# Two layers of a transformer encoder on one core: the down projection of pairs 2 to 7 in blocks of seven products

## The reference, cut to what matters

```python
for l in range(DEPTH):                       # DEPTH = 2
    xp = xp + token_mix(rmsnorm(xp, norm_mix[l]), ...)
    xp = xp + swiglu(rmsnorm(xp, norm_ffn[l]), w_ff_gate[l], w_ff_up[l], w_ff_down[l])
def swiglu(h, wg, wu, wd):
    return (jax.nn.silu(h @ wg) * (h @ wu)) @ wd
```

## Time and profile before

| | |
|---|---|
| Time, median of three runs | 2314.57 us |
| Time of the profiled execution | 2312.65 us |
| Its span, first to last instruction | 2310.9 us |
| PE busy | 98% of the span |
| DVE, ACT, POOL busy | 56%, 37%, 43% |
| Feed-forward stages | about 719 to 1156 us and 1860 to 2294 us |
| Mean granted TensorE clock | 0.997 of full speed |

### The profile page before, as it was taken

How to read it: one execution, slowest core, us unless ns; L and a number is a source line. 1 busy time by engine, 2 the same in 40 slices (tenths; PEclk the granted TensorE clock), 3 DMA queues, 4 the chain that set the end, 5 groups by cost and what they waited for, 6 DMA issues and landing times.

```text
span 2310.9 us, 39749 instructions
## 1 busy us (share of the span) xinstructions
PE 2262.2 (98%) x15086; PEld 2178.7 (94%) x15086; DVE 1305.1 (56%) x2330; ACT 847.1 (37%) x1650; POOL 988.0 (43%) x992
## 2 busy tenths in 40 slices
PE   8999999999999999999999999999999999999997
PEld 7998998888999999999999999978889999999997
DVE  7998553334226935727589975433332477275374
ACT  4115233444213534525420152334442245254352
POOL 5554454222564342333465445532326643333231
PEclk9999999999999999999999999999999999999998
DMA  5351121111223222322244411211112322223121
GB/s 193 104 175 62 51 73 55 37 40 35 91 100 97 68 92 65 96 70 84 65 137 149 122 56 57 70 51 37 38 42 92 109 87 83 72 84 100 65 86 61
DMA packets 70565, 187.87 MB, mean 81 GB/s; under 512 B 19824, under 2 KB 22480, under 8 KB 69392
## 3 DMA queue, kind: packets, MB, share of 16 engines
q1 hardware_dynamic: 62608, 165.64, 22.7%
q10 hardware_dynamic: 7808, 20.16, 2.6%
HBM read 173.47 MB, written 14.14 MB: 81 GB/s over the span
## 4 chain that ended last, share of the span: by engine, by line
PE 81%; DVE 16%; issue 2%; ACT 1%; DMA 0%; SPq 0%; DVEq 0%; ACTq 0%
PE gemm L712 37%; PE gemm L1182 16%; PE gemm L1172 13%; DVE side L1959 7%; PE side L1182 3%; PE side L1172 2%; PE side L1055 2%; PE side L1035 1%; PE side L818 1%; PE side L986 1%; PE side L1042 1%; DVE prod L1868 1%; DVE h_lo L1822 1%; DVE act L2298 1%; DVE act_lo L2308 1%
## 5 line engine op out<-in xcount | busy, mean ns | idle before, releaser
L685 POOL TENSOR_TENSOR ring_lo<-w_raw,ring_hi 128x512 fp32r<-128x512 f32 x236 | 319.5, 1357 | 552.4 <-ACT ring_hi L1648 552.4
L666 POOL CAST w_hi<-w_raw 128x384 fp32r<-128x384 f32 x376 | 222.8, 593 | 711.4 <-PE gemm L712 667.3
L668 POOL TENSOR_TENSOR w_lo<-w_raw,w_hi 128x384 fp32r<-128x384 f32 x376 | 450.1, 1197 | 30.1
L712 PE MATMUL gemm<-h_hi,w_hi 128*128 128x320 f32 x1616 | 405.9, 332 | 5.0 <-DVE h_lo L1822 3.8
L712 PE MATMUL gemm<-h_hi,w_lo 128*128 128x320 f32 x1616 | 368.9, 309 | 0.0
L712 PE MATMUL gemm<-h_lo,w_hi 128*128 128x320 f32 x1616 | 368.4, 309 | 0.0
L712 PEld LDWEIGHTS gemm<-h_hi,w_hi 128*128 128x128 f32 x1616 | 274.1, 189 | 36.6 <-issue 17.2
L712 PEld LDWEIGHTS gemm<-h_hi,w_lo 128*128 128x128 f32 x1616 | 270.5, 188 | 0.0
L712 PEld LDWEIGHTS gemm<-h_lo,w_hi 128*128 128x128 f32 x1616 | 270.5, 188 | 0.0
L1182 PE MATMUL gemm<-act_hi,ring_hi 128*128 128x320 f32 x864 | 267.2, 309 | 1.1 <-DVE prod L2285 1.1
L1182 PE MATMUL gemm<-act_hi,ring_lo 128*128 128x320 f32 x864 | 267.0, 309 | 0.0
(11 more groups left out here) (330 smaller groups left out, 4387.9 us busy)
## 6 DMA issues: line engine op xcount, KB each, us to landing
w_raw<-in_ws_ff SPq DMA_DIRECT2D x120, 512.0 KB, 3.4
w_raw<-in_ws_gate SPq DMA_DIRECT2D x64, 512.0 KB, 3.4
w_raw<-in_ws_in SPq DMA_DIRECT2D x44, 512.0 KB, 3.5
w_raw<-in_ws_proj SPq DMA_DIRECT2D x64, 256.0 KB, 2.6
w_raw<-in_ws_out SPq DMA_DIRECT2D x16, 512.0 KB, 3.4
w_raw<-in_ws_fd SPq DMA_DIRECT2D x16, 384.0 KB, 3.1
x_park<-x ACTq DMA_DIRECT2D x2, 2560.0 KB, 12.4
x<-x_park ACTq DMA_DIRECT2D x4, 1280.0 KB, 5.9
```

What stands on the lines that cost most here:

```text
L666: eng.tensor_copy(w_hi[s][:, cols], w_raw[s][:, cols]).then_inc(w_high.sem, 1)
L668: eng.tensor_tensor(w_lo[s][:, cols], w_raw[s][:, cols], w_hi[s][:, cols].bitcast(F32), ALU.subtract).then_inc(w_split.sem, 1)
L685: eng.tensor_tensor(lo, src, hi.bitcast(F32), ALU.subtract).then_inc(lo_plain.sem, 1)
L712: mm = eng.matmul(dst[:, hf, 0:HALF], w, r[k][:, cols] if r in (xu_hi, xu_lo) else r[:, k, cols], start=first and k == 0 and part == 0, st ...
```

## The change

The flow of the feed-forward part becomes a table, `FF_FLOW`: the gate and up blocks of pair 2; the plain down units of tiles 0 to 3; pairs 3 and 4; four **down blocks** over pairs 2, 3, 4; pairs 5, 6, 7; four down blocks over pairs 5, 6, 7; pairs 8, 9, 10; the plain down units of tiles 16 to 21.

A down block computes two output tiles (2i and 2i+1) from three pairs, by seven products. Its inner dimension is three tiles for each half, so a product is 3 x 3 = 9 matmuls and a block 63; its operands have 384 columns, not 512. Its activation blocks are made of f: for each of pairs 2 to 7 the end of the up block now makes four sums of f (S3, S1, S2, S4, VectorE, 128x320), seven high parts (ScalarE) and seven low parts (three on GpSimd: A11, A22, A12; four on VectorE), in place of two high and two low parts of 128x640. Which engine makes the low part of a weight operand is also a table, `POOL_OPS`: in gate and up blocks GpSimd keeps operands 0 and 3, and operand 6 goes to VectorE; in down blocks GpSimd has 0, 3, 4 and 6.

```diff
-FF_CHUNKS = (8, 8, 6)
+FF_FLOW = (("pair", 2), ("units", 0, 4), ("pair", 3), ("pair", 4), ("downs", (2, 3, 4)),
+           ("pair", 5), ("pair", 6), ("pair", 7), ("downs", (5, 6, 7)),
+           ("pair", 8), ("pair", 9), ("pair", 10), ("units", 16, 6))
+POOL_OPS = {"gate": (0, 3), "up": (0, 3), "down": (0, 3, 4, 6)}
...
 # TensorE
+    def block_product(v, i, dst, name, fresh):
+        tiles, wh, wl = weights(v.n + i)
+        for k in range(tiles):
+            if v.kind == "down":
+                hi, lo = f_hi[v.pairs[k], name][:, :], f_lo[v.pairs[k], name][:, :]
+                if v.out == 0 and name in POOL_LOWS:
+                    eng.wait_ge(block_pool.sem, ...)
+                elif v.out == 0:
+                    eng.wait_ge(block_dve.sem, ...)
...
 # ScalarE, quad(v): follows = the block before is an up block of pairs 2 to 7, split = this one is
     copied(QX, QY)
     cast(n + 5)
+    if follows:
+        block_high_made(b.pair, A12)
...
     copied(QW, QZ)
     cast(n + 6)
+    if follows:
+        block_high_made(b.pair, S1)
+        block_high_made(b.pair, S4)
...
     cast(n + 9)
+    if split:
+        block_high_made(v.pair, A11)
     done(5)
     cast(n + 10)
+    if split:
+        block_high_made(v.pair, A22)
+        block_high_made(v.pair, S3)
     done(6)
     cast(n + 11)
+    if split:
+        block_high_made(v.pair, S2)
...
 # VectorE, quad(v)
-    if more:
-        weight_sums(q + 1, False)
-    sum_low(n + 5)
-    if more:
-        weight_sums(q + 1, True)
+    next_sums(v, False)
+    operand_low(n + 5)
+    late_lows(v)                 # low parts of S1 and S4 of the pair before
+    next_sums(v, True)
+    operand_low(n + 6)
...
+        if split:
+            block_summed(pair, S3)
+            block_summed(pair, S1)
+            block_summed(pair, S2)
         done(6)
         eng.tensor_tensor(fb[1][:, lo_half], gb[1][:, lo_half], QV, ALU.mult).then_inc(ff_value.sem, 1)
+        if split:
+            block_low(pair, S3)
+            block_summed(pair, S4)
+    next_low(v, n + 11)
+    if split:
+        block_low(pair, S2)
...
+def down_quad(v):
+    next_sums(v, False)
+    operand_low(n + 5)
+    late_lows(v)
+    next_sums(v, True)
+    copied(2); added(QW, m + 1, hi_half)
+    copied(4); added(u2, m, hi_half)
+    done(3);   added(QX, m, lo_half)
+    next_low(v, n + 8)
+    copied(5); added(u4, m + 1, hi_half)
+    next_low(v, n + 9)
+    done(5);   added(QZ, m, hi_half)
+    next_low(v, n + 11)
+    done(6);   added(QV, m + 1, lo_half)
```

More of the change, by code:

```diff
@@ L133, in _ff_operands, with __init__ @@
+class Load:
+    def __init__(self, tiles, halves):
+        self.tiles, self.halves, self.pool, self.dve = tiles, halves, 0, 0
+class Quad:
+    def __init__(self, kind, n, index, nk, pair=None, out=None, pairs=None):
+        self.kind, self.n, self.index, self.nk = kind, n, index, nk
+        self.pair, self.out, self.pairs = pair, out, pairs
+        self.g = self.units = 0
+        self.before = self.after = None
 def _ff_operands():
     ops, loads, quads, units = [], [], [], []
-    plain = sums = 0
@@ L138, in add @@
[L138 to L141, removed]
-        else:
-            sums += 1
-        ops.append(Operand(load, part, cols, summed, plain if summed is None else sums))
+    pool = dve = 0
+    def add(load, start, cols, by_pool, summed=None, quad=None):
+        nonlocal pool, dve
+        if by_pool:
+            pool += 1
+            loads[load].pool = pool
+        else:
+            dve += 1
+            loads[load].dve = dve
+        ops.append(Operand(load, start, cols, summed, by_pool, pool if by_pool else dve, quad))
@@ L146, in unit @@
     def unit(tiles):
-        r = len(loads)
+        loads.append(Load(tiles, 1))
         units.append(len(ops))
[L149 to L182, removed]
+        first = min(4, (tiles + 1) // 2) if tiles < 6 else 4
+        add(len(loads) - 1, 0, first * P, True)
@@ new lines, in _ff_operands @@
+    for _ in range(4 * PLAIN):
+        unit(KT)
+    q = d = 0
+    last, units_since = None, len(units)
+    for step in FF_FLOW:
+        new = []
+        if step[0] == "pair":
+            for k, kind in enumerate(("gate", "up")):
+                new.append(Quad(kind, len(ops) + 7 * k, q, 4, pair=step[1]))
+                q += 1
+        elif step[0] == "downs":
+            for i in range(KT // 2):
+                new.append(Quad("down", len(ops) + 7 * i, d, len(step[1]), out=i, pairs=step[1]))
+                d += 1
+        else:
+            for _ in range(KT):
+                unit(step[2])
+            units_since = len(units)
+        for v in new:
+            v.g, v.before, v.units = len(quads), last, units_since
+            if last is not None and not units_since:
+                last.after = v
+            last, units_since = v, 0
+            quad(v)
@@ L183 @@
+    return ops, loads, quads, units, pool, dve, q, d
+FF_OPS, FF_LOADS, FF_QUADS, FF_UNITS, N_POOL, N_DVE, N_PAIRED, N_DOWNS = _ff_operands()
 N_QUADS, N_FF_UNITS = len(FF_QUADS), len(FF_UNITS)
-FF_STREAM = len(FF_LOADS) - KT
+GATE_UP = {(v.pair, v.kind): v for v in FF_QUADS if v.kind != "down"}
+DOWNS = {(v.pairs, v.out): v for v in FF_QUADS if v.kind == "down"}
 USES = FF_G0 + N_FF_UNITS // 2
+N_FULL = sum(1 for a in FF_LOADS if a.tiles * a.halves == KT)
+N_DOWN3 = sum(1 for a in FF_LOADS if a.halves == 2) - 2 * N_PAIRED
@@ L631, in _ @@
                              layer_of(io["ws_out"], l * KT + i * 2 + s), UW)
-                for r, (width, _, _) in enumerate(FF_LOADS):
+                full, down, narrow = l * N_FULL, l * N_DOWN3, l * KT
+                last = l * KT
+                for r, load in enumerate(FF_LOADS):
                     if r < 2:
@@ L1742, in quad @@
                     done(3)
-                    if not up:
+                    if gate:
                         silu_block(QX, gb[0][:, lo_half])
@@ new lines, in next_low, with late_lows, quad @@
+                def next_low(v, n):
+                    if v.after is not None:
+                        operand_low(n)
+                def late_lows(v):
+                    b = v.before
+                    if b is not None and not v.units and b.kind == "up" and b.pair in SPLIT_PAIRS:
+                        block_low(b.pair, S1)
+                        block_low(b.pair, S4)
+                def quad(v):
+                    n, q, pair, up = v.n, v.index, v.pair, v.kind == "up"
+                    split = up and pair in SPLIT_PAIRS
```

462 lines of the change are left out of this document (305 added, 157 removed).

## The result

The changed kernel took 2318.9 us (median of 14 runs), the kernel before 2314.6 us (14 runs beside them). The ratio is 1.002, with a 95% interval of 1.0012 to 1.0028. The forecast was 1.9 us less; it became 4.3 us more. The profiled execution took 2318.65 us. One of the 14 runs took 4425.1 us, and the comparison leaves it out (the median of the other 13 is 2318.65).

What follows compares the result with a forecast made beforehand. TensorE, busy 98% of the span, was taken as the bound. 21.1 us saved against 19.2 us of stalls gave -1.9 us, so 2310.7 for the profiled execution and 2312.7 us median; 8-in-10 range 2298 to 2320.

Steps and rivals of the forecast that it cites:

- the saving: Down projection of pairs 2 to 7: 144 matmuls less at 0.1467 us each, 21.1 us saved.
- The rival of another pace: Down blocks: products of nine matmuls run slower than those of twelve, by a fixed cost per product; no time or chance given.
- where the waits are: First down blocks, products 1 and 4, 2 to 4 us together; gate blocks, products 2, 5, 6, 0.3 to 1.5 us.
- Bounds 0 and 3.7; I take 3.0: Up block then down block, 4 times: TensorE stalls 3.0 us each, waiting for VectorE's low parts of S3 and S1.
- The ledger: Instructions of three engines laid side by side at block ends: stalls of up to 3.7 us (down) and 1.2 us (gate).
- as at 761 us: Down transition: if VectorE keeps its turn against GpSimd once, the stall is 2.05 us instead of 3.7.
- Sum 1.2 us: Up block then gate block, 6 times: copy QX to QY 0.4, operand 5 0.5, operand 6 0.3 us; bounds 0 and 2.0.
- 19.2: Total forecast stalls in us at the ends of up blocks: 4 x 3.0 + 6 x 1.2, against 21.1 saved.
- the slower rival: Down and gate blocks behind up blocks: the port decides, 2323.5 us, deciding from 25.7 us of stalls; chance 0.18.
- its price of 30 us: Slower case's stalls when VectorE waits for whole, drawn-out GpSimd instructions: 4 x 4.5 + 6 x 2.0 us.

Runs made afterwards that it cites:

- e2: Changed kernel with GpSimd's feed-forward low parts filled with zero instead of subtracted, their share left out of the result; 2291.03 us, ratio 0.9903.
- e9: Changed kernel with GpSimd's feed-forward low parts as zero fills without reads, each cut into eight pieces; 2290.78 us, ratio 0.9899.
- e10: Changed kernel with f work late in gate blocks, and pair 5's (8's) gate block placed between pair 4's (7's) up block and the down blocks; 2291.66 us.
- e6: Changed kernel with the edits of e4 and e5 together: late f work and reordered down transition; 2308.88 us, ratio 0.9984.
- e8: As e6, with the fourth weight sum behind the first three additions to x in the first down block; 2307.72 us, ratio 0.998.
- e4: Changed kernel with sums and parts of f made late in the gate block that follows an up block, on all three engines; 2311.56 us, ratio 0.999.
- e3: Changed kernel with low parts of operand 5, S1 and S4 ahead of the weight sums in the first down block; 2316.98 us, ratio 1.0011.
- e5: Changed kernel with e3's order, S3's low part ahead of the sum S2, and GpSimd's A22 last; 2322.57 us, ratio 1.0042.
- e1: Changed kernel with the low part of operand 6 in gate and up blocks back on GpSimd; 2324.78 us, ratio 1.0051.
- e7: Kernel before the change, with only operand 6's low part in gate and up blocks moved from GpSimd to VectorE; 2313.87 us, ratio 0.9998.

## Why the prediction was wrong

**Held: the saving.** 144 matmuls less, and 0.1467 us between matmuls in products of nine as in those of twelve: between its waits the down block runs at that pace. The rival of another pace falls with it. e2, e9 and e10, with hardly a wait or none in the blocks, are 22.8, 21.9 and 23.4 us below the kernel before, where 21.1 is the matmuls' share (e2 and e9 also lose the first block's wait, 1.6 us in all).

**Held: where the waits are.** The waits for the low parts of f are at products 1 and 4 of the first down block, four times, and in the gate blocks of pairs 4, 6 and 7 at products 2, 5 and 6. There are none in the later down blocks, in the units, behind pair 2 or behind loads, and the first block is unchanged. A stall gives VectorE time, so nothing adds up from block to block.

**Failed: "Bounds 0 and 3.7; I take 3.0".** This is the term of the up block followed by a down block. It measured 4.0, above my upper end. The ledger had the two stalls nearly right: 1.3 and 2.4 us laid out (2.3 by its own times, 22.1 - 18.48 - 1.3), 1.49 and 0.36 + 1.90 measured, before restarts. What failed is the 0.7 that I took off it for the case that VectorE keeps its turn once, as at 761 us (and at 1899 us, the same place in the second layer): in the stretch above GpSimd came next at all four boundaries from 887.7 us on. The sum leaned on one event; that VectorE can keep its turn is real (e6 and e8 show it in the first block), but it did not do so here. And each restart of TensorE costs 0.07 to 0.10 us more at the second matmul (0.25 between starts for 0.147), which I had not counted. 4 x 1.0 = 4.1 us of the miss.

**Failed: "Sum 1.2 us" for the gate transition.** It measured 1.6. Without restarts it would be 1.3: the copy 0.57 where I had 0.4 (once 0.90), operand 5 0.43 where I had 0.5, operand 6 0.23 where I had 0.3. Three restarts make 0.27. 2.2 us of the miss.

**Not in the sum: the clock.** 1.5 us for a down transition at which it falls. In the blocks it was seen only behind the stalls of product 4.

**What this does to the sign.** 19.2 became 25.5. The stalls had to stay under 21.1 for any gain, and the forecast stood 1.9 us from that point, with two terms of 4 and 6 repeats: 0.2 us in each transition would have turned it. The ledger's own numbers (3.7 and 1.2) give 22.0; with the 30 restarts (some 2.8 us) they give 24.8, and 0.7 is left. The measured 25.5 is just short of the 25.7 from which the slower rival was to decide. Its mechanism, the port, is the right one; its price of 30 us was too high.

**Shown and not shown.** That GpSimd's reads stretch VectorE's instructions, and that the waits for VectorE go with them, is shown by e2, within the limit of e9: it was not tried with fills as long as the subtraction. For the start of product 4 (1.7 of the 25.5 us) the cause is inferred from the times. That a block of room removes them with the reads in place is shown by e4 and e10. The fall of the clock is seen in the profiled executions alone: behind none of the four down transitions in e3, e5, e6 and e8, one in the changed kernel, two in e1 and e4. The profiled executions also show falls to 0.50 at other places without these stalls (583.8 us in e6, 1149.5 in e2, 1724.9 in e7). The spread of the timed runs doesn't settle what the falls cost there: it is 9.1 us in e4 and 4.0 in the changed kernel, and 6.5 in the kernel before, which has no such stalls. Nothing shows how much of a median is clock.

## What to carry to other kernels

Where three engines with lists in order feed a TensorE that never waits, cost new work at the place where its result is due, not by the engine's busy share: here VectorE was idle for more than a quarter of the time in the blocks before the change, and its results came 0.2 to 1.9 us late where it counted. If a ledger of durations gives a number, use it; don't take something off for luck seen at one place. And when a transition is full, don't reorder it (by the profiles a down transition lost 4.0 us before any reordering, 3.8 in e3, 4.1 in e5 and e6, 4.0 in e8); put a block of other work between the block that finishes the input and the block that uses it (e4 won 7, e10 27).

## What the runs showed of the hardware

- In the transitions VectorE waited for one whole instruction of GpSimd at a boundary. The same 128x320 sum (L2501 `f_block<-prod`) takes 0.49 us in e2 and 1.30 us (mean of 12) in the changed kernel. The Trainium skill (SBUF — State Buffer, Who interferes with whom) gives the lock to whoever issues first; the traces agree where the two alternate, but not everywhere. At 761 us in the kernel before and at 776.08 and 777.48 us in e6 VectorE's instructions start later than the waiting one of GpSimd and go first. Who gets a boundary is thus not fixed by the order in the lists: the same place of the program went to GpSimd in the changed kernel and to VectorE in e6 and e8. What decides it no run here shows.
- A fill on GpSimd does not hold VectorE up: in e9 fills ran at the same places in pieces, and VectorE's low parts of f stayed at 485 to 486 ns.
- Stalls can cost more than their length. The granted clock fell to 0.50 at 2150.7 us, behind stalls of 1.6, 0.4 and 2.0 us in one block, and rose again at 2154.1 us, when matmuls had run without a gap; in the other three down transitions the same stalls left it at 1.00.
- The first block's waits, already there before the change, have the same cause: they are gone in e2 and e9, where GpSimd doesn't read, and in e6 and e8, where it reads and VectorE kept its turn.
